# A two-layer transformer stack with routed experts: the two expert outputs of a row are added on the way into memory, by an accumulating transfer that Pool issues

## What is computed

```python
def hier_moe(h, ...):
    ...                                # each row picks its two best experts of 32
    ys = lax.map(run, (xs, block_e)).reshape(-1, d_)
    return jnp.zeros_like(h).at[slot_tok].add(ys * slot_gate[:, None])
...
    y = hier_moe(tokens, ...)
    if not last:
        ctx = layer_norm(ALPHA * ctx + mod_c[5] * y[b_ * s_:]..., ln2_g[l], ln2_b[l])
    x = layer_norm(ALPHA * x + g2 * y[:b_ * s_]..., ln2_g[l], ln2_b[l])
```

## Time and profile before

| | us |
|---|---|
| median of 3 runs | 3165.96 |
| lowest, highest | 3161.48, 3169.25 |
| time of the profiled execution | 3160.6 |
| its span (first to last instruction) | 3158.8 |
| PE busy in it | 2755.3 (87%) |
| DVE busy in it | 1079.2 (34%) |
| Pool busy in it | 320.9 (10%) |

### The profile page before, as it was taken

One profiled execution on the slowest core, in us unless ns is written; L12 is line 12 of the kernel. 1 busy time (PEld: TensorE's weight loads), 2 busy tenths in 40 slices (PEclk: granted clock), 3 DMA queues, 4 the chain that ended last, 5 costly groups with the idle time before them and its releaser, 6 DMA issues.

```text
span 3158.8 us, 33588 instructions
## 1 busy us (share of the span) xinstructions
PE 2755.3 (87%) x11408; PEld 1258.6 (40%) x11408; DVE 1079.2 (34%) x2096; ACT 457.9 (14%) x846; POOL 320.9 (10%) x446
## 2 busy tenths in 40 slices
PE   6999969999998999999599978873999688999773
PEld 3444424444444446564533322222555433333221
DVE  3998960330003042454531111117244521111114
ACT  2111132100011010540100100001052100011000
POOL 0101012000000000000122211110000221222110
PEclk9999989999999999999599999986999699999886
DMA  6655521211220311000789999965100699779993
GB/s 214 205 189 193 173 107 55 96 64 69 80 80 0 117 54 49 5 12 31 262 329 373 380 393 393 389 240 194 56 26 23 240 359 382 277 264 364 392 373 134
DMA packets 272211, 603.02 MB, mean 191 GB/s; under 512 B 18437, under 2 KB 43333, under 8 KB 272001
## 3 DMA queue, kind: packets, MB, share of 16 engines
q1 hardware_dynamic: 256864, 580.70, 50.5%
q0 software_dynamic: 15264, 21.24, 1.9%
HBM read 743.04 MB, written 29.20 MB: 244 GB/s over the span
## 4 chain that ended last, share of the span: by engine, by line
PE 69%; SPq 12%; DMA 7%; DVE 6%; issue 3%; ACT 2%; POOL 0%; POOLq 0%; DVEq 0%; ACTq 0%
PE psum L1309 11%; PE psum L969 11%; PE psum L1018 10%; SPq L620 10%; PE psum L1146 9%; PE psum L990 7%; DMA arena<-in_w 5%; PE psum L1331 4%; PE psum L1241 4%; PE psum L1193 2%; PE psum L1182 1%; PE psum L954 1%; PE psum L1039 1%; PE psum L1256 1%; PE psum L1205 1%
## 5 line engine op out<-in xcount | busy, mean ns | idle before, releaser
L1309 PE MATMUL psum<-arena 128*64 128x512 f32 x2656 | 647.3, 633 | 117.3 <-DMA arena<-in_w 115.7
L1309 PEld LDWEIGHTS psum<-arena 128*64 128x64 f32 x2656 | 196.0, 144 | 448.4 <-issue 443.2
L969 PE MATMUL psum<-arena 128*128 128x512 f32 x768 | 344.1, 601 | 2.8 <-ACT arena L700 2.8
L1018 PE MATMUL psum<-arena 128*128 128x512 f32 x768 | 329.9, 592 | 0.8 <-ACT arena L692 0.8
L1406 DVE SCALAR_TENSOR_TENSOR arena<-arena 128x512 f32<-128x512 f32 x464 | 308.7, 745 | 0.0
L1331 PE MATMUL psum<-arena 128*64 128x512 f32 x1328 | 301.9, 598 | 0.0
L1146 PE MATMUL psum<-arena 128*128 128x512 f32 (+1 forms) x800 | 288.9, 523 | 5.9 <-issue 4.0
L990 PE MATMUL psum<-arena 128*128 128x512 f32 x512 | 225.3, 603 | 11.1 <-POOL arena L2049 10.4
L1018 PEld LDWEIGHTS psum<-arena 128*128 128x128 f32 x768 | 145.8, 190 | 184.2 <-issue 183.2
L969 PEld LDWEIGHTS psum<-arena 128*128 128x128 f32 x768 | 142.5, 190 | 174.2 <-issue 174.2
L1146 PEld LDWEIGHTS psum<-arena 128*128 128x128 f32 x800 | 153.2, 193 | 134.7 <-issue 125.0
(11 more groups left out here) (269 smaller groups left out, 2123.5 us busy)
## 6 DMA issues: line engine op xcount, KB each, us to landing
arena<-in_w SPq DMA_DIRECT2D x261, 2048.0 KB
arena<-in_w_ada SPq DMA_DIRECT2D x48, 1024.0 KB, 5.2
arena<-in_conv_w_in SPq DMA_DIRECT2D x24, 1024.0 KB
arena<-in_ret_w_in SPq DMA_DIRECT2D x12, 2048.0 KB, 8.1
arena<-in_w_in SPq DMA_DIRECT2D x8, 2048.0 KB, 8.3
arena<-moe_out SPq DMA_DIRECT2D x10, 1024.0 KB, 9.8
arena<-in_conv_w_out SPq DMA_DIRECT2D x4, 2048.0 KB, 10.3
arena<-in_ret_w_out SPq DMA_DIRECT2D x4, 2048.0 KB, 7.7
```

The costliest lines, as they stand in the source:

```text
L969: m = pe.matmul(bank(b + c), w[:, k, c * P:(c + 1) * P], c_hT[:, k, :], start=(k == 0), stop=(k == KD - 1))
L1018: m = pe.matmul(bank(4 * (n % 2) + j), l_, r_, start=(k == 0), stop=(k == KD - 1))
L1309: m = pe.matmul(bank(2 * s)[part], m_xsT[s][:, at:at + SB], m_w[s][j][:, k, :], start=(k == 0), stop=(k == KD - 1))
```

## The change

SP no longer brings the expert outputs back. It waits for `m_done` and raises it once more, to tell Pool that its own waits are over (it waits for the last weights of all streams ahead of that, since `c_y` takes their place). Pool, after raising `m_done` itself, waits for SP's, brings the first output of every tile with a plain transfer of 512 KB, and then, tile by tile, waits until the first output has landed and issues a second transfer of 512 KB that adds the second output to it in place. DVE's addition is gone; it waits until both transfers of a tile have landed (`32 * (l + 1)` of `cg`) and begins with the multiplication by the gate.

```diff
@@ SP
-                sp.wait_ge(sem("m_done"), l + 1)
-                for t in full(l):
-                    sp.dma_start(c_y[t], moe_out[l].rearrange("(k t p) d -> t p k d", k=2, p=P)[t])\
-                        .then_inc(sem(f"cg{t}"), 16)
+                sp.wait_ge(sem("m_done"), 2 * l + 1)
+                sp.sem_inc(sem("m_done"), 1)
@@ DVE, combine
-                    y0, y1 = c_y[t][:, 0, :], c_y[t][:, 1, :]
-                    dve.wait_ge(sem(f"cg{t}"), 16 * (l + 1))
-                    link(dve.tensor_tensor(y0, y0, y1, ALU.add))
+                    y0 = c_y[t][:, 0, :]
+                    dve.wait_ge(sem(f"cg{t}"), 32 * (l + 1))
                     link(dve.tensor_tensor(y0, y0, b_mod[int(t >= TX)], ALU.mult))
@@ Pool
                 pool.sem_inc(sem("m_done"), 1)
+                pool.wait_ge(sem("m_done"), 2 * l + 2)
+                outs = moe_out[l].rearrange("(k t p) d -> k t p d", k=2, p=P)
+                for t in tiles:
+                    pool.dma_start(c_y[t][:, 0, :], outs[0, t]).then_inc(sem(f"cg{t}"), 16)
+                for t in tiles:
+                    pool.wait_ge(sem(f"cg{t}"), 32 * l + 16)
+                    pool.dma_start(c_y[t][:, 0, :], outs[1, t], accum_op=ALU.add).then_inc(sem(f"cg{t}"), 16)
```

## The result

The changed kernel takes 3177.44 us (median of 7 runs, 3171.1 to 3178.43), the one before 3165.12 us beside it (7 runs): 12.3 us slower, a ratio of 1.0041 with a 95% interval of 1.003 to 1.0051. The forecast was 5.2 us slower, too little to be told from no change; the loss is more than twice that and can be told.

What follows compares the result with a forecast made beforehand. In seam and tail, tile 0's transfer latency and then DVE's own work were taken to bound the kernel. Tail -0.3 and seam +5.5 us gave +5.2: 3165.96 + 5.2 = 3171.2 us, range 3163 to 3188.

Steps and rivals of the forecast that it cites:

- rival 1: Seam and tail: accumulating transfer slow, DVE follows the transfers; +13.1 us at 5.0 us a tile, 3179; chance 0.32.
- DVE's addition goes: Ten additions on the chain at 1.25 us each: 7.5 us saved in the seam, 5.0 in the tail.
- Price (a): Pool's own time for each new transfer: 1.0 us, taken from its indirect transfers over 128 partitions.
- Price (d): Accumulating transfer of 512 KB a tile: 2.5 us for its data, range 1.25 to 5.0.
- Price (b): Each Pool transfer's latency from issue to landing without the data: 3.25 us, Pool's time in it.
- Queueing in the tail: Tail: tile 0's sum issued at 3121.6, landing after 3.25 + 2.5 us, no wait behind the other loads counted.
- Price (e): Hand-over from Pool to SP and back: the way back estimated at 0.2 us.
- Tail: Layer 1's end: tile 0 comes 4.7 us later, less 5.0 for the additions, so -0.3 us.
- Seam: Between layers: tile 0 comes 13.0 us later, behind six loads beside the weights, less 7.5, so +5.5 us.
- At nothing: SP's saved issues, the weights' later end, Pool's memset and tiles after the first: hidden, no cost.
- Rival 2: Seam: the accumulation doesn't queue behind the loads, or Pool's queue is served first; -0.3 us in all, 3165.7; chance 0.12.
- Rival 3: Seam: weights win, with half the bytes each six loads take 15.7 us, +4 on the forecast, 3175; chance 0.08.

Runs made afterwards that it cites:

- e7: The kernel before without DVE's addition, the second output left out of the sum: ratio 0.9964 to the kernel before.
- e8: Changed kernel, but SP brings the first outputs ahead of the weights and Pool only issues the accumulating transfers: ratio 0.9997 to the kernel before.
- e2: Changed kernel, but SP issues the next layer's weights only when the last tile's sum has landed: ratio 1.0024 to the kernel before.
- e3: Changed kernel with Pool's plain loads and accumulating transfers interleaved, one load ahead of the first sum: ratio 1.0025 to the kernel before.
- e4: Changed kernel, but Pool brings both outputs of a tile in one plain 1 MB transfer and DVE adds: ratio 1.0023 to the kernel before.

## Why the prediction was right or wrong

The direction and the range (3163 to 3188) were right. The likeliest case was not: it stood for 5.2 us, "same", and 12.3 us is slower beyond what a measurement can tell, the case that had 0.40. That the time still lies in the range is in part luck: the range reached up to 3188 for a slow sum (rival 1, 3179 at 5.0 us a tile), and the sum was not slow. By its steps:

- **DVE's addition goes, 12.5 us:** right. The steps are 1.25 us shorter in the trace, and e7 gives 12.5 us in seam and tail.
- **Price (a), 1.0 us of Pool's time for each:** too high for the plain ones (0.55 to 0.59 us), near for the accumulating (0.86 to 0.91). It had the nearest row wrong: the 0.60 us of direct transfers, not the 1.02 of indirect ones.
- **Price (d), the data of an accumulating transfer, 2.5 us:** right, 1.68 MB in 8 us, 210 GB/s.
- **Price (b), latency without data, 3.25 us:** this is the step that failed, in the seam. Beside SP's busy queue the start of a Pool transfer alone takes about 4 us (changed, e8), and the first load landed after 7.1 us (3.25 + 1.93 = 5.2 forecast); with SP's queue idle it landed after 3.8 (e2). In the tail the price held: the first load landed after 3.82 us with its data (4.5 forecast), and in e3, with one load ahead of the sum, DVE began 5.56 us after the sum's issue (3131.15 to 3136.71), where 5.75 stood for latency and data.
- **Queueing in the tail, at nothing:** this failed too. The sum issued at 3129.43 took 7.9 us where 5.75 stood, because it stood behind three loads. They were ahead of it by the prediction's own times as well (the last load issued by 3121.1, the sum at 3121.6); it counted this queueing in the seam alone. e3 takes 2.6 us of it back.
- **Price (e), the hand-over, 0.2 us:** 0.47 us (2141.41 to 2141.88), and another 0.49 us from tile 0's landing to the issue of its sum (3128.94 to 3129.43), which no term had.
- **Tail, -0.3 us:** +2.3. Tile 0 came 7.0 us later, not 4.7.
- **Seam, +5.5 us:** +8.0. Tile 0 came 15.6 us later, not 13.0; the missing 2.6 us are Pool's late start beside the weights (7.1 us to the first landing, not 5.2) and the hand-over. The mechanism is shown by e2 (the weights), e3 (the order in the queue) and e4 (Pool's queue), each of which takes some of it back. The split of two thirds to one third was nearly right: 3.05 and 1.80 MB.
- **At nothing:** held. Later tiles hid, the weights came in time even when issued 32.4 us after the scatter instead of 4.8 (e2), and Pool's memset, started at 2159.93, was over at 2161.65, long before the projection.
- **Rival 1 (a slow sum, 5 us a tile):** not it; the tiles came at DVE's pace. Rival 2 (no queueing) fell in the trace. Rival 3 (+9.5 us in the seam) comes nearest to the seam's 8.0, but the time was lost by latency and not by the weights' share. Two to four microseconds elsewhere had no rival at all.

## What to carry to other kernels

Work on the critical path that is moved to a transfer pays the transfer's latency once for the first tile and saves its own time once for each tile. So leave the first tiles on the fast path and give the transfer those that have time to wait: here two of each layer's tiles on DVE and the rest accumulated, with all first outputs brought by SP, turned 12 us lost into 5.5 us gained. And when an issue moves from one queue to another, look at what it used to hold back: SP's weights stood behind the outputs in one queue, and beside them in two.

## What the runs showed of the hardware

An accumulating transfer of 512 KB from device memory into on-chip memory moved 210 GB/s alone, half of the 421 of plain ones that SP issued. The Trainium skill's page "Collectives: The Full Stack", section "The bandwidth ceiling", says of the adding transfers of a ReduceScatter that they reach about half the rate of copies, since an addition reads two sources. The trace agrees on the half; the two reads no run here shows.

From issue to landing an accumulating transfer took 7.8 us in e8's tail and 9.7 us in its seam, both beside a busy queue of SP's, and 5.4 us at the least in e3's tail, where SP's queue was idle. What I hadn't expected is the start. Beside SP's busy queue no packet of Pool's moved for over 4 us after the issue in the seam (changed, e8) and for 3.2 us in e8's tail; with SP's queue idle it was under 1.5 us (e2).

Pool itself was busy for 0.56 us with a plain transfer of 128 runs and for 0.86 us with an accumulating one.
